# Attention loops that wait by halves of four heads, and a router whose logits come from rows before the norm

## What is computed

```python
logits = jnp.einsum('bdhnqc,bdhnkc->bdhnqk', qb, kb) * scale + bias[None, None, :, None]
logits = jnp.where(valid, logits, -jnp.inf)
m = jnp.max(logits, axis=-1)
p = jnp.exp(logits - m[..., None])
s = jnp.sum(p, axis=-1)
num = jnp.einsum('bdhnqk,bdhnkc->bdhnqc', p, vb)
```

## Time and profile before

| what | us |
|---|---|
| median of 3 timed runs | 2952.6 (2950.39 to 2957.13) |
| profiled execution | 2939.17, of which span 2937.4 |
| attention loop, group 1 (928.6 to 992.2 of the span) | 63.6 |
| attention loop, group 2 (1128.0 to 1192.6) | 64.6 |
| attention loop, group 3 (1332.9 to 1383.5) | 50.6 |
| last projection, second half from the first step on (2504.1 to 2551.9) | 47.8 |
| router after the last tile (2551.9 to 2574.2) | 22.3 |

### The profile page before, as it was taken

One profiled execution on the slowest core, in us unless ns is written; L12 is line 12 of the kernel. 1 busy time (PEld: TensorE's weight loads), 2 busy tenths in 40 slices (PEclk: granted clock), 3 DMA queues, 4 the chain that ended last, 5 costly groups with the idle time before them and its releaser, 6 DMA issues. The chain is left out here.

```text
span 2937.4 us, 40180 instructions
## 1 busy us (share of the span) xinstructions
PE 2706.2 (92%) x16278; PEld 2207.7 (75%) x16278; DVE 1481.4 (50%) x2201; ACT 1058.1 (36%) x1868; POOL 378.6 (13%) x360
## 2 busy tenths in 40 slices
PE   8999999999899998998799999998999999949997
PEld 5777777777677888797677778867888777838786
DVE  5225543333373414213845242027666664579997
ACT  4114411111223414215226322115666521227775
POOL 0005400000120000001301000013111011113431
PEclk9999999999999999998899999999999999969999
DMA  7554661212321202203634112210000064269997
GB/s 220 200 191 134 186 192 49 74 57 63 109 100 37 80 15 48 83 0 120 199 115 153 47 43 90 85 62 20 2 1 1 3 196 141 115 240 360 378 378 257
DMA packets 261859, 355.96 MB, mean 121 GB/s; under 512 B 54091, under 2 KB 173027, under 8 KB 260268
## 3 DMA queue, kind: packets, MB, share of 16 engines
q1 hardware_dynamic: 212700, 201.17, 21.6%
q0 software_dynamic: 33744, 127.05, 13.3%
q10 hardware_dynamic: 15232, 25.17, 2.4%
HBM read 281.25 MB, written 76.80 MB: 122 GB/s over the span
## 5 line engine op out<-in xcount | busy, mean ns | idle before, releaser
L230 PE MATMUL ps<-h_hi,st_w_lo 128*128 128x512 f32 x880 | 363.7, 413 | 14.1 <-PEq L821 5.7
L232 PE MATMUL ps<-h_hi,st_w_hi 128*128 128x512 f32 x880 | 346.5, 394 | 0.0
L231 PE MATMUL ps<-h_lo,st_w_hi 128*128 128x512 f32 x880 | 346.4, 394 | 0.0
L227 DVE TENSOR_TENSOR ew_lo<-wraw,ew_hi 128x1024 fp32r<-128x1024 f32 x192 | 223.0, 1217 | 9.0 <-ACT ew_hi L224 8.2
L230 PEld LDWEIGHTS ps<-h_hi,st_w_lo 128*128 128x128 f32 x880 | 167.6, 190 | 65.8 <-issue 34.1
L224 ACT ACTIVATE ew_hi<-wraw 128x1024 fp32r<-128x1024 f32 x192 | 191.6, 1057 | 21.5 <-DMA wraw<-w_e_gate 9.2
L232 PEld LDWEIGHTS ps<-h_hi,st_w_hi 128*128 128x128 f32 x880 | 166.9, 190 | 36.1
L231 PEld LDWEIGHTS ps<-h_lo,st_w_hi 128*128 128x128 f32 x880 | 167.6, 190 | 32.5 <-issue 2.4
L227 DVE TENSOR_TENSOR st_w_lo<-wraw,st_w_hi 128x1024 fp32r<-128x1024 f32 x64 | 90.7, 1417 | 179.5 <-ACT st_w_hi L224 178.8
L230 PE MATMUL ps<-h_hi,w_ring_lo 128*128 128x512 f32 (+1 forms) x336 | 134.7, 401 | 2.5 <-DVE h_lo L227 1.5
L231 PE MATMUL ps<-h_lo,w_ring_hi 128*128 128x512 f32 (+1 forms) x336 | 133.6, 398 | 0.0
(11 more groups left out here) (587 smaller groups left out, 6363.0 us busy)
## 6 DMA issues: line engine op xcount, KB each, us to landing
wraw<-w_in SPq DMA_DIRECT2D x98, 512.0 KB, 4.9
wraw<-w_e_gate SPq DMA_DIRECT2D x64, 512.0 KB, 12.6
wraw<-w_e_up SPq DMA_DIRECT2D x64, 512.0 KB, 14.0
wraw<-w_e_down SPq DMA_DIRECT2D x64, 512.0 KB, 13.4
mod_w<-w_mod POOLq DMA_DIRECT2D x12, 2048.0 KB, 9.5
gates<-st_zo ACTq DMA_DIRECT2D x48, 256.0 KB, 2.0
rw_in<-rw_scan POOLq DMA_DIRECT2D x8, 1280.0 KB, 6.4
wraw<-w_out SPq DMA_DIRECT2D x16, 512.0 KB, 5.4
```

The source lines that it names most:

```text
L227: return dve.tensor_tensor(dst, src, hi.bitcast(F32), ALU.subtract)
L230: pe.matmul(out, a[1], b[0], start=first, stop=False)
L231: pe.matmul(out, a[0], b[1], start=False, stop=False)
L232: return pe.matmul(out, a[0], b[0], start=False, stop=last)
```

## The change

It has two parts. In the **attention loops** the bias, the maximum and the exponentials of a block are done and waited for in two halves of four heads. VectorE's list interleaves them with its copies; the transposes of a half wait for that half's exponentials alone. For blocks with two key tiles `output` holds 64 columns of `v` stationary, for two heads in turn in the two 64-column halves of the array, and moves the probabilities, so that the numerators come out transposed; ScalarE copies them, TensorE turns them back with four transposes (`back`), and ScalarE copies them again (`by_token`). For blocks with one key tile the numerators are as before, and VectorE copies them (`token_rows`) instead of ScalarE. In the **router** the transposes read `x2` before the norm. The weights are multiplied by the gain once, on GpSimd, and held stationary in four column blocks of 32 that each sum a quarter of the channels; ScalarE copies the four parts, a matmul with a 0/1 matrix adds them, and the row scale and the term of the shift are applied to the logits in the next stage. The modulated rows are still made and written, each tile one step earlier, and three steps follow the last tile instead of five. One more group of semaphores is retired (`c_in`), and the row scale lives in `gains`. The diff, cut; removed lines stand in the functions above where they are left out here:

```diff
                 def scores(pe, j):
                     if j:
-                        pe.wait_ge(sn["sb"], bs["sb"] + j)
+                        pe.wait_ge(sn["sb"], bs["sb"] + 2 * j)
...
+                    if par == 0:
+                        if j == 0:
+                            dve.wait_ge(sn["bias"], bs["bias"] + 32)
+                        dve.wait_ge(sn["sc"], bs["sc"] + j + 1)
+                        if j >= 2:
+                            dve.wait_ge(sn["tr"], bs["tr"] + gsum[j - 1])
+                    dve.scalar_tensor_tensor(
+                        sbuf[:, j % 2, par, :, w:], ps[:, 2 * par:2 * par + 2, :].rearrange(
+                            "p a (b k) -> p (a b) k", b=2)[:, :, w:], 0.125,
+                        bias[:, par, :, w:], ALU.mult, ALU.add).then_inc(sn["sb"], 1)
+
+                def row_max(dve, j, par):
+                    w = 2 * P - nkey[j] * P
+                    if par == 0 and (j >= 3 or g):
                         dve.wait_ge(sn[f"out{j % 3}"], bs[f"out{j % 3}"] + 16 * (j // 3))
+                    dve.wait_ge(sn["sb"], bs["sb"] + 2 * j + par + 1)
+                    dve.tensor_reduce(og[:, j % 3, 520 + par:528:2], sbuf[:, j % 2, par, :, w:], X, ALU.max, negate=True
                                       ).then_inc(sn["nm"], 1)
...
+                    for par in range(2):
+                        act.wait_ge(sn["nm"], bs["nm"] + 2 * j + par + 1)
+                        for hh in range(4):
+                            h = 2 * hh + par
+                            part = sbuf[:, j % 2, par, hh, w0:]
+                            e = act.activation(part, part, ACT.Exp, bias=og[:, j % 3, 520 + h:521 + h],
+                                               accum_out=og[:, j % 3, 512 + h:513 + h])
+                        e.then_inc(sn["exp"], 1)
...
+                        for par in range(2):
+                            biased(dve, 0, par)
+                            row_max(dve, 0, par)
...
+                                pe.wait_ge(sn[f"pt{x}"], bs[f"pt{x}"] + done[j + 1])
                             if j:
+                                pe.wait_ge(sn["og"], bs["og"] + done[j])
+                            if nkey[j] == 1:
+                                for h in range(HEADS):
+                                    mm = pe.matmul(ps[:, 7, h * HD:(h + 1) * HD], pt[:, j % 2, 0, h % 2, h // 2, :],
+                                                   v[:, j, h * HD:(h + 1) * HD], start=True, stop=True)
+                                mm.then_inc(sn["pv"], 1)
+                                return
+                            for m in range(4):
+                                for kb in range(2):
+                                    for a in range(2):
+                                        h = 2 * m + a
+                                        mm = pe.matmul(ps[HD * a:HD * a + HD, 7, m * P:(m + 1) * P],
+                                                       v[:, j - 1 + kb, h * HD:(h + 1) * HD], pt[:, j % 2, kb, a, m, :],
+                                                       start=(kb == 0), stop=(kb == 1))
                             mm.then_inc(sn["pv"], 1)
+
+                        def back(j):
+                            if nkey[j] == 1:
+                                return
+                            pe.wait_ge(sn["og"], bs["og"] + done[j] + 1)
+                            for m in range(4):
+                                tr = pe.transpose(ps[:, 7, m * P:(m + 1) * P], og[:, j % 3, m * P:(m + 1) * P], ident[:, :])
+                            tr.then_inc(sn["pv"], 1)
...
-                            pe.wait_ge(sn["exp"], bs["exp"] + j + 1)
                             for n in range(ngrp[j]):
-                                kb, par = n // 2, n % 2
+                                par, kb = divmod(n, nkey[j])
...
+                                pe.wait_ge(sn["exp"], bs["exp"] + 2 * j + par + 1)
...
-                                    pe.wait_ge(sn[f"pt{(w - 3) % 2}"], bs[f"pt{(w - 3) % 2}"] + (w - 3) // 2 + 1)
+                                    pt_copied(pe, w - 3)
...
+                            if j:
+                                back(j - 1)
                         output(NT - 1)
+                        back(NT - 1)
...
+                        def token_rows(j):
+                            dve.wait_ge(sn["pv"], bs["pv"] + done[j + 1])
+                            dve.tensor_copy(og[:, j % 3, 0:512], ps[:, 7, :]).then_inc(sn["og"], 1)
+
...
+                                biased(dve, j + 1, 0)
+                                row_max(dve, j + 1, 0)
+                            if nkey[j] == 2:
+                                turned(j, 0)
+                            if j + 1 < NT:
+                                biased(dve, j + 1, 1)
+                            if j and nkey[j - 1] == 1:
+                                token_rows(j - 1)
+                            turned(j, 3 if nkey[j] == 2 else 1)
+                            if j + 1 < NT:
+                                row_max(dve, j + 1, 1)
                         if ahead:
                             ahead_low(dve, 0, ahead[0], slots[0])
+                        if nkey[NT - 1] == 1:
+                            token_rows(NT - 1)
...
-                            act.wait_ge(sn["pv"], bs["pv"] + j + 1)
-                            act.activation(og[:, j % 3, 0:512], ps[:, 7, :], ACT.Copy).then_inc(sn["og"], 1)
+                            if nkey[j] == 2:
+                                act.wait_ge(sn["pv"], bs["pv"] + done[j] + 1)
+                                act.activation(og[:, j % 3, 0:512], ps[:, 7, :], ACT.Copy
+                                               ).then_inc(sn["og"], 1)
+
+                        def by_token(j):
+                            if nkey[j] == 2:
+                                act.wait_ge(sn["pv"], bs["pv"] + done[j + 1])
+                                act.activation(og[:, j % 3, 0:512], ps[:, 7, :], ACT.Copy).then_inc(sn["og"], 1)
...
-                            for n in range(0, ngrp[j], 2):
+                            for n in ((1, 2) if nkey[j] == 2 else (0,)):
+                                par, kb = divmod(n, nkey[j])
...
+                            if j:
+                                by_token(j - 1)
...
-                            sp.wait_ge(sn["og"], bs["og"] + j + 1)
+                            sp.wait_ge(sn["og"], bs["og"] + done[j + 1])
...
                     gp.dma_start(wr[:, :, :], A["w_router_2"][0].rearrange("(k p) e -> p k e", p=P)).then_inc(S("n4_in"), 16)
-                    for s_ in range(NT + 2):
+                    gp.memset(wf[:, :, :], 0.0).then_inc(S("n4_wf"), 1)
+                    gp.wait_ge(S("n4_in"), 48)
+                    gp.wait_ge(S("n4_wf"), 1)
+                    gp.tensor_tensor(wf[:, :, 0:NE], wr[:, :, :], gains[:, 5, :].unsqueeze(2).to_broadcast([P, KD, NE]),
+                                     ALU.mult).then_inc(S("n4_wf"), 1)
+                    for s_ in range(NT + 1):
                         if s_ < NT:
                             gp.wait_ge(S("r2_x"), s_ + 1)
                             gp.dma_start(out[0, s_ * P:(s_ + 1) * P, :], x2[:, s_, :]).then_inc(S("fi_out"), 16)
-                        if s_ >= 2:
-                            t = s_ - 2
+                        if s_ >= 1:
+                            t = s_ - 1
                             gp.wait_ge(S("n4_h"), t + 1)
                             gp.dma_start(xn_d[t * P:(t + 1) * P, :], hrow[:, t % 3, :]).then_inc(S(f"n4_out{t % 3}"), 16)
...
                 def pe_step(pe, s_):
                     t = s_ - 3
                     if 0 <= t < NT:
-                        pe.wait_ge(S("n4_h"), t + 1)
+                        pe.wait_ge(S("n4_copied"), t + 1)
+                        pe.matmul(ps[:, 3, t * NE:(t + 1) * NE], quarters[:, t % 2, :], pick[:, :], start=True, stop=True
+                                  ).then_inc(S("n4_l"), 1)
+                    t = s_ - 2
+                    if 0 <= t < NT:
+                        if t == 0:
+                            pe.wait_ge(S("n4_in"), 48)
+                            pe.wait_ge(S("n4_wf"), 2)
+                            for k in range(KD):
+                                pe.matmul(ps[:, 3, P:P + NE], gains[:, 6, k:k + 1].to_broadcast([P, P]), wr[:, k, :],
+                                          start=(k == 0), stop=(k == KD - 1))
+                        for b in range(2):
+                            pe.wait_ge(S(f"n4_ev{b}"), t + 1)
+                        o = 2 * P + P * (t % 2)
+                        for k in range(KD):
+                            q_ = 32 * (k % 4)
+                            mm = pe.matmul(ps[q_:q_ + 32, 3, o:o + P], wf[:, k, :], ht[:, t % 2, k, :],
+                                           start=(k < 4), stop=(k >= 4))
+                        mm.then_inc(S("n4_part"), 1)
+                    t = s_ - 1
```

(39 more changed lines are left out.)

125 lines of the change are left out of this document (39 added, 86 removed).

## The result

| kernel | median, us | before on the same chip, us | ratio (95% interval) |
|---|---|---|---|
| changed | 2916.6 | 2951.5 | 0.9887 (0.9859 to 0.9916) |
| changed, measured again | 2916.9 | 2944.9 | 0.9894 (0.9872 to 0.9916) |

That is 28 to 35 us less, where 20 were forecast, and 2916.6 lies under the range (2920 to 2949). The profiled execution fell only from 2939.2 to 2915.2; for it the forecast was 2919. The rest lies in the kernel before: 83 timed executions of it, over all comparisons, run from 2936 to 2965 with a median of 2948. Its profiled execution was among the quicker ones, and the three behind the forecast's median of 2952.6 were among the slower ones. The ten of the changed kernel lie between 2912 and 2922.

What follows compares the result with a forecast made beforehand. TensorE, busiest engine in the attention loops, was taken as the bound, VectorE's 6.45 us block as the next. Loops -6, -5, -2 and router -7 make -20 us: 2952.6 to 2932.6, own range 2924 to 2943, 8 in 10 2920 to 2949.

Steps and rivals of the forecast that it cites:

- more: Rival, attention loops: half waits also remove the stops at the loops' ends and the clock holds; -31 us, 2922; chance 0.10.
- all the ends together: Whole kernel: the extreme ends of the loop and router terms summed, giving 2951.6 us or 2921.0 us.
- the block: Loop 1, scores to scores: 7.47 us falls to 6.45, set by VectorE's chain, with TensorE at 6.24.
- the rival that they would not: Rival, loops and router: two-block passes don't overlap, numerators stay at 3.63 us; about 2954; chance 0.04.
- The opening's later second scores: Loop 1: first scores after the opening come 1.25 us later, the second bias half standing behind a maximum.
- The rule of the Trainium skill: Loops 1 and 2: tiling speeds up matmuls but not evacuation; by it, extra evacuation takes the whole gain.
- evacuation takes the gain: Rival, loops 1 and 2: waits in ScalarE's chain keep the block at 7.4 us; 2943.6; chance 0.18.
- the router, -7 forecast: Router: last tile ends 2.9 us later, stage closes 11.5 us after it (E), softmax gets two more operations; net -7 us.
- the tails of the loops: Loop ends: only loop 2's tail gains, about -1.2 us, second half's exponentials running beside the first half's transposes.
- the clock falls: Rival, attention loops: TensorE, with fewer passes while waiting, drops to the lower clock; some +50 us, 2983; chance 0.06.
- The same edit there gives 2932.6: Whole kernel: -20 us carried from the profiled execution (2919) to the timed median of 2952.6, 13.4 above it.
- loop 2's stop: Loop 2: write behind `res_gates` still lands at 1149, scores move from 1148.5 to about 1151.5; earlier gains lost there.

Runs made afterwards that it cites:

- two-block, old order: New router with the attention loops of before, changed only to two-block numerators with transposes back and a second ScalarE copy in two-key-tile blocks: 2938.3 us, ratio 0.9952.
- idle transposes: Kernel before plus unit-matrix transposes in TensorE's waits of each attention loop's last two blocks: 2938.0 us, ratio 0.9972; same edit in the changed kernel: 2913.8 us, 0.9874.
- first trace of before: Profiled execution of the unchanged kernel from which the forecast was made: 2939.2 us (span 2937.4).
- second trace of before: Another profiled execution of the unchanged kernel, one of its longest: span 2963.1 us, 25.7 more than the first; that kernel's timed median then was 2950.9.

## Why the prediction was wrong in size

The sign and the parts were right, the sum too small: 2916.6 is beyond even the rival "more" (2922) and all the ends together (2921). As a difference, the 28 to 35 us measured stand around the 31 of "more", which had a chance of 0.10.

**Right:** the block, in part by luck. Loop 1 was set by TensorE and came down to 6.40. The 6.45 forecast was VectorE's chain (its terms as written add up to 6.48), with TensorE at 6.24 beside it. In the trace it is TensorE that has no hole: its transposes and transposes back take 2.57, not 2.40. VectorE, which was to have no idle time, waits 0.38 and is done 0.05 ahead of the next scores. Numerators take 1.90 for 32 passes (1.92), so the two-block passes do overlap as in the earlier trace rows and the rival that they would not is out. The opening's later second scores are there (5.7 us after the first instead of 4.6; 1.25 forecast). Transposes back cost 0.57, not 0.48. The rule of the Trainium skill (TensorEngine Tiling (Array Packing), section PSUM Bottleneck) did not decide here; the page names a speedup of four, and the numerators got 1.9 times faster. With the halves the second evacuation fits beside TensorE's 6.40, and ScalarE even waits 0.41. With whole waits (two-block, old order) TensorE waits 0.79 a block for ScalarE's exponentials, and ScalarE in turn 0.26, 0.27 and 0.32 for TensorE ahead of three of its copies: the chain of waits that the rival "evacuation takes the gain" described. So that rival was real, and the halves kept it off.

**Right, by terms that made up for each other:** the router, -7 forecast, 4 to 6 us by the medians. Logits took 0.57 a tile (0.7 taken), and the last tile's projection ended 1.6 us later than before (49.4 us from the first step on instead of 47.8), not 2.9. The tail went by the steps told: squares at E + 2.4, the last modulating pass done at E + 7.3, the write landed at E + 10.6. But the stage closed at E + 13.6, not 11.5. Between the landing at 2547.6 and the next stage lies a drain of the Pool engine of 2.50 us (2547.87 to 2550.37 in the trace), a term that the sum did not have; before, it lay beside TensorE's logits. With the write off the Pool queue the drain runs from 2542.93 to 2545.35, ahead of the landing at 2545.9, and the stage closes at E + 10.3. Of these 3.3 us 2.6 lie behind the landing, which shows the drain, and 0.7 ahead of it.

**Wrong: the tails of the loops.** This is the step that failed. The working had -1.2 us for the loops' ends, in loop 2 only, and left the rest to the rival "more"; the ends gave 12 to 19. One reason is the halves: in the last blocks nothing else fills TensorE, so that each wait for half of the heads shortens the chain itself. The other is the clock, which I had as a loss (the rival "the clock falls") or at best as holding ("more"). The 0.84 and 0.80 of the earlier trace rows stood there before the change; I read them as a state that the change could worsen, not as time that it could give back. The idle transposes show that 8 us of it can be had without shortening any work.

The table of tails gives an estimate of how the two divide. With the clock up nearly throughout, the old tails take 20.1 us in loop 1 (first trace of before) and 19.8 and 16.7 in loops 2 and 3 (idle transposes); the changed ones take 18.2, 16.8 and 14.9. So about 7 us of the tails' gain are shorter work and waits. The other 5 us against the first trace of before, and 12 against the second, are the clock. How the 7 divide between halves and numerators stays open.

**Wrong: carrying the edit from the profiled execution to the median.** "The same edit there gives 2932.6" took the 13.4 us between the two as a constant. There were two faults in it. The 2952.6 was the median of three executions; that of all 83 is 2948. And part of what makes executions differ is what the change acts on: in the second trace of before the lower clock has 23 us more in the three windows, and the loops take 9 us more. The other 17 of the 25.7 us between the traces lie outside the loops, so the loops explain a part of the spread, and what the rest hangs on stays open. A sum made on a quick execution is too small for the median in so far as the edited stretch is what varies.

**Wrong, smaller:** loop 2's stop. I had the write of the record landing at 1149 whatever the loop does, and 3 us behind it. It landed earlier (the maximum starts at 1143.95 after 1.51 us of waiting, 18.6 us into the loop instead of 21.0), for the last piece of weights ahead of it had landed 13.4 us into the loop instead of 17.5. That is not the change's doing: in the second trace of before the piece had landed 14.3 us in, and the record 18.6 instead of 20.9. The 1149 came from the slowest of all traces here. The loop's fourth scores start 21.0 us in, instead of 20.5 (23.5 forecast). After it a pair of blocks takes 11.0 us instead of 12.9, a gain of 1.9, not 1.23. In loop 3 the stop grew from 4.63 to 7.00 us, for the most part because VectorE got there earlier: the maximum starts 16.2 us into the loop instead of 15.4 (the sum had 0.7 for this stop). It ate the loop's gain up to the last scores, against the first trace of before.

## What to carry to other kernels

Cost the end of a loop by itself: there the engines overlap less, more of the waits lie on the path, and the bound that was read from a steady block need not hold. Where executions of one kernel differ by more than the edit is worth, find out in which stages they differ before carrying a sum from one profile to the median; an edit in such a stage can gain or lose more than its own work. A shorter matmul and a finer wait can be worth little alone (9 and 7 us here, the router's 5.6 taken off) and much together (27), so a test that undoes one of two parts does not give the other's share.

## What the hardware showed

TensorE's clock differs between executions of one unchanged kernel: 65 and 88 of 255 us at 1.2 GHz in the same three windows, and 27 with idle transposes in its stops. In the router's stage a drain of the Pool engine of 2.50 us began only after that engine's wait for its last write had ended, and the stage closed behind it. A write of the same row tile that ScalarE's queue issued and waited for landed 2.6 us after its issue, and the stage closed 0.4 later. In loop 2 the first record landed 18.1 to 20.9 us into the loop in the thirteen traces with two small writes ahead of it on the queue, and 15.6 us in the one without.
